# A two-dimensional Fourier step folded by the symmetries of cosine and sine

## The reference, cut to what matters

```python
f_in, f_gate, q_a, kv_a, k_pe, m_gate = split_cols(h_lat @ w_in, EVEN_SPLITS)
...
def fourier_mix(u):
    b, n, _ = u.shape
    f = jnp.fft.fft2(u.reshape(b, n, F_GROUPS, F_GROUP_DIM).astype(jnp.float32), axes=(1, 3), norm='ortho')
    return f.real.reshape(b, n, F_WIDTH).astype(u.dtype)
...
y_l = jnp.concatenate([fourier_mix(f_in) * jax.nn.silu(f_gate),
                       a_l.reshape(b, n, MLA_WIDTH) * jax.nn.silu(m_gate)], axis=-1) @ w_out
```

## Time and profile before

| | us |
|---|---|
| median of 3 runs | 1409.98 |
| lowest, highest | 1406.64, 1414.62 |
| span of the profiled execution (first to last instruction) | 1407.9 |
| PE busy | 1332.3 (95%) |
| DVE busy | 952.2 (68%) |
| ACT busy | 498.6 (35%) |

### The profile page before, as it was taken

One profiled execution on the slowest core, in us unless ns is written; L12 is line 12 of the kernel. 1 busy time (PEld: TensorE's weight loads), 2 busy tenths in 40 slices (PEclk: granted clock), 3 DMA queues, 4 the chain that ended last, 5 costly groups with the idle time before them and its releaser, 6 DMA issues.

```text
span 1407.9 us, 19069 instructions
## 1 busy us (share of the span) xinstructions
PE 1332.3 (95%) x7945; PEld 1087.6 (77%) x7945; DVE 952.2 (68%) x1229; ACT 498.6 (35%) x752; POOL 149.9 (11%) x167
## 2 busy tenths in 40 slices
PE   6999999999999899999998999998999999899997
PEld 2589756546885549889887989886989988789895
DVE  3667857656558576597689666657657778755546
ACT  0422125403246223533232443433354333343432
POOL 2010110000000010012322000002001232100000
PEclk9999999999999999999999999999999999999998
DMA  9453562024331356676774676654557776355551
GB/s 358 150 183 114 176 209 90 19 102 158 126 107 44 121 180 231 195 268 222 278 263 153 236 259 220 202 179 152 188 200 254 269 273 221 122 185 197 184 180 60
DMA packets 104910, 257.95 MB, mean 183 GB/s; under 512 B 8213, under 2 KB 11766, under 8 KB 104570
## 3 DMA queue, kind: packets, MB, share of 16 engines
q1 hardware_dynamic: 80554, 171.78, 36.1%
q0 software_dynamic: 20192, 75.58, 14.8%
q10 hardware_dynamic: 4080, 9.39, 2.0%
HBM read 255.68 MB, written 1.05 MB: 182 GB/s over the span
## 4 chain that ended last, share of the span: by engine, by line
PE 70%; DVE 16%; DMA 4%; ACT 4%; issue 3%; POOL 1%; ACTq 1%; SPq 0%; POOLq 0%; DVEq 0%
PE bank L758 68%; DMA weight_ring<-in_w_in_dram 3%; DVE weights_low L2110 2%; PE bank L918 2%; DMA x<-in_ctx_dram 1%; ACT odd_prob L1694 1%; DVE negated_maxima L2321 1%; POOL inverse_roots L661 1%; ACT weights_high L1521 1%; DVE statistics L2064 1%; ACT even_A L1639 1%; DVE x L2063 1%; DVE xn L2057 1%; DVE x L2552 1%; DVE modulation_sums L1922 1%
## 5 line engine op out<-in xcount | busy, mean ns | idle before, releaser
L2110 DVE TENSOR_TENSOR weights_low<-weight_ring,weights_high 128x2048 fp32r<-128x2048 f32 (+1 forms) x124 | 272.5, 2200 | 227.2 <-ACT weights_high L1521 227.1
L1521 ACT ACTIVATE weights_high<-weight_ring 128x2048 fp32r<-128x2048 f32 (+1 forms) x124 | 227.5, 1836 | 391.2 <-PE bank L758 302.4
L758 PE MATMUL bank<-uT_high,weights_high 128*128 128x256 f32 (+1 forms) x1200 | 341.2, 284 | 8.6 <-DVE weights_low L2110 3.1
L758 PE MATMUL bank<-uT_low,weights_high 128*128 128x256 f32 (+1 forms) x1200 | 339.5, 283 | 0.0
L758 PE MATMUL bank<-uT_high,weights_low 128*128 128x256 f32 (+1 forms) x1200 | 339.4, 283 | 0.0
L758 PEld LDWEIGHTS bank<-uT_high,weights_high 128*128 128x128 f32 (+1 forms) x1200 | 228.3, 190 | 14.1 <-ACT gate_tanh L1835 7.2
L758 PEld LDWEIGHTS bank<-uT_low,weights_high 128*128 128x128 f32 (+1 forms) x1200 | 228.5, 190 | 1.0
L758 PEld LDWEIGHTS bank<-uT_high,weights_low 128*128 128x128 f32 (+1 forms) x1200 | 228.4, 190 | 0.5
L1922 DVE SCALAR_TENSOR_TENSOR modulation_sums<-modulation_ring,silu_c_columns,modulation_sums 128x1024 f32<-128x1024 f32 x112 | 148.7, 1327 | 20.5 <-DMA modulation_ring<-in_w_ada_dram 11.1
L758 PE MATMUL bank<-weights_high,hidden_high 128*128 128x512 f32 x256 | 102.4, 400 | 1.9 <-DVE weights_low L2110 1.9
L758 PE MATMUL bank<-weights_low,hidden_high 128*128 128x512 f32 x256 | 101.8, 398 | 0.0
(11 more groups left out here) (303 smaller groups left out, 2202.5 us busy)
## 6 DMA issues: line engine op xcount, KB each, us to landing
weight_ring<-in_w_in_dram SPq DMA_DIRECT2D x52, 1024.0 KB, 6.7
modulation_ring<-in_w_ada_dram POOLq DMA_DIRECT2D x48, 1024.0 KB, 7.3
weight_ring<-in_w_up_dram SPq DMA_DIRECT2D x32, 1024.0 KB, 5.4
weight_ring<-in_w_down_dram SPq DMA_DIRECT2D x32, 1024.0 KB, 5.0
modulation_ring<-in_w_mod_dram POOLq DMA_DIRECT2D x16, 1024.0 KB, 5.9
weight_ring<-in_o_w_in_dram SPq DMA_DIRECT2D x10, 1024.0 KB, 5.2
weight_ring<-in_w_branch_dram SPq DMA_DIRECT2D x16, 512.0 KB, 3.8
weight_ring<-in_w_o_dram SPq DMA_DIRECT2D x8, 1024.0 KB, 7.0
```

The lines of the kernel that those rows point to most:

```text
L758: return track(pe.matmul(*args, **kw))
L1521: act.activation(ring[:, s, c0:kn * cols], wring[:, slot, c0:kn * cols], ACT.Copy).then_inc(S["high_ready"], 1)
L2110: dve.tensor_tensor(lo[:, s, c0:kn * cols], wring[:, slot, c0:kn * cols], hi[:, s, c0:kn * cols].bitcast(F32), ALU.subtract).then_inc(w_fr ...
```

## The change

Cosine is even and sine is odd in both indices. So (1) f1 computes only 65 cosine columns (0 to 64) and 63 sine columns (1 to 63), 128 together, and ACT writes the others as mirror images, with the sign turned for sine. (2) Tokens t and 256 - t have the same cosine and opposite sine: fin's copy writes tokens 1 to 128 as they are and then 255 down to 128 in reversed order, f1 adds or subtracts the two halves in the accumulator (two products, the second with the sine columns negated), and f2 sums over 128 tokens instead of 256. (3) Token 0 is apart: one product f0 with 8 columns (4 groups times 2 streams), in bank 7; DVE copies it to `dft0` and adds it per partition when it reads f2, one instruction for each stream, since the scalar differs. (4) DVE's `gemv` calls are placed anew: gemv(3, 0) ahead of f2(0), gemv(3, 1) ahead of f2(2), gemv(3, 2), gemv(3, 3) and gemv(4, 0) behind f2(3), and gemv(4, 1..3) behind `mod_columns(3)`. f2 stays in bank 6 alone.

```diff
@@ first_jobs
+        if g == 0:
+            jobs += [(("f0",), last)]
         if g < 4:
-            jobs += [(("f1", g, h), (4, 5)) for h in range(2)]
+            jobs += [(("f1", g), (4, 5))]
...
@@ PE
+            for m in range(4):
+                copied(("fin", m))
+            o = start(("f0",))
+            first_tokens = fT.rearrange("p g s n -> p (g s) n")[:, :, 0]
+            done(product(o[:, 0:8], kE[:, KE_ALL:KE_ALL + P], first_tokens, start=True, stop=True), ("f0",))
             for g in range(5):
                 if g < 4:
-                    copied(("fin", g))
...
+                    o = start(("f1", g))
+                    for s in range(2):
+                        for part in range(2):
+                            ins = product(o[:, P * s:P * s + P], fT[:, g, s, P * part + 1:P * part + P + 1], kE[:, KE_CH + P * part:KE_CH + P * part + P],
+                                          start=(part == 0), stop=(part == 1), skip_group_check=True)
+                    done(ins, ("f1", g))
...
                     for s in range(2):
-                        for i in range(TC):
-                            for part in range(2):
...
+                        for part in range(2):
+                            seq = KE_SEQ + N * part
+                            ins = product(o[:, N * s:N * s + N], dft1[:, (g - 1) % 2, s, P * part:P * part + P],
+                                          kE[:, seq:seq + N], start=(part == 0), stop=(part == 1),
+                                          skip_group_check=True)
@@ ACT
-                copy_out(("fin", m), fT[:, m, :], o[:, :])
+                act.activation(fT[:, m, :, 0:P + 1], o[:, :, 0:P + 1], ACT.Copy)
+                copy_out(("fin", m), fT[:, m, :, P + 1:N + 1], o[:, :, N - 1:P - 1:-1])
...
+                act.activation(dst[:, :, 0:EVENS], o[:, :, 0:EVENS], ACT.Copy)
+                act.activation(dst[:, :, EVENS:P], o[:, :, EVENS - 2:0:-1], ACT.Copy)
+                act.activation(dst[:, :, P + 1:P + EVENS - 1], o[:, :, EVENS:P], ACT.Copy)
+                copy_out(("f1", g), dst[:, :, P + EVENS:2 * P], o[:, :, P - 1:EVENS - 1:-1], scale=-1.0)
@@ DVE
+            link(dve.memset(dft1[:, :, :, P], 0.0))
+            link(dve.memset(dft1[:, :, :, P + EVENS - 1], 0.0))
             low_e("fgate", 0)
...
+            o = ready(("f0",))
+            ins = dve.tensor_copy(dft0, o[:, 0:8])
+            release(ins, ("f0",))
+            copied(("f0",))
             for g in range(4):
-                gemv(3, g)
+                if g % 2 == 0:
+                    gemv(3, g // 2)
...
-                if g == 1:
-                    mod_columns(2, mcol, 0)
-            for q in range(3):
-                gemv(4, q)
+            mod_columns(2, mcol, 0)
+            for q in range(2, 4):
+                gemv(3, q)
+            gemv(4, 0)
             for m in range(4):
                 gated_tile(("mgate", m), 4 + m, eyT[:, 4 + m, :], tanh_e[:, m % 2, :])
             mod_columns(3, mcol, 1, vcol[:, V_NG + KD:V_NG + 2 * KD])
-            gemv(4, 3)
+            for q in range(1, 4):
+                gemv(4, q)
```

54 lines of the change are left out of this document (24 added, 30 removed).

## The result

The changed kernel takes 1422.2 us (median of 4 runs, 1417.9 to 1422.6), the kernel before beside it 1412.1 (4 runs, 1406.6 to 1414.6): a ratio of 1.0076, 95% interval 1.0058 to 1.0095. It is slower by 0.8%. The profiled execution spans 1420.2 us, against 1407.9.

What follows compares the result with a forecast made beforehand. It took DVE, not PE, to pace the stage: 3.8 us gained up to mgate, 6.0 lost behind it and 3.9 lost to PE's lower clock made +6.1 on the median 1409.98, so 1416, range 1405 to 1422.

Steps and rivals of the forecast that it cites:

- f0's copy: On DVE after the low part of mgate: copying f0 was put at 0.2 us, within 0.1 to 0.3.
- The wait of about 5 us: Sign that the forecast is right: PE waits about 5 us in the stage for DVE's reading of f2(0).
- mgate at 148.3: End of the stage: DVE's terms sum to 16.8 us, so mgate starts at 148.3 instead of 152.10, 3.8 us gained.
- half the clock in f2(1): After PE's 6.8 us wait for bank 6, f2(1) probably runs at half the clock: +1.5 us (0 to 1.7).
- Behind mgate: +6.0: From mgate to qb's second half: three late quarters make it 46.3 us against 40.3, 6.0 us lost.
- the ring: Behind mgate: DVE waits for the third late quarter's data, whose slot the first of them frees, 0.7 us (0 to 3).
- the three waits for which the prediction had a term: PE's waits ahead of f2(1), f2(3) and qb's second half lower the clock: +1.5, +0.8 and +1.6, together +3.9 us.
- The 5.0: Clock cost by the Trainium skill's rule, under which all three PE waits cost: 5.0 us instead of 3.9.
- PE's gain arrives: Rival for the stage: PE is at 95%, and 13.6 us come off, giving 1396; chance 0.06.
- The late quarters are hidden: Rival behind mgate: the late quarters do not reach qb and the 3.8 us gain stays, 1406; chance 0.08.
- DVE's pace without falls of the clock: Rival: no wait lowers PE's clock, leaving +2.2 us, 1412; chance 0.12.
- Slower by the ring: Rival behind mgate: last quarter's transfer lands late, clock stays low into kvb, +2 each: +10, 1420; chance 0.14.

Runs made afterwards that it cites:

- e1: The changed kernel with f0 copied out of bank 7 by ACT, ahead of its f1 loop, instead of by DVE; 1415.6 us, ratio 1.0041.
- e12: The changed kernel with f0 written to bank 6 instead of bank 7, still copied by DVE; 1417.7 us, ratio 1.0041.
- e4: The kernel before, without the fold, with only the changed kernel's new places of DVE's gemv quarters; 1417.2 us, ratio 1.0056.
- e6: Against e3: one bank for f1, two for f2, f0 in bank 6, DVE's quarters put off behind the readings of f2; 1401.2 us, ratio 0.9918.
- e10: Folded kernel with e6's quarter places and ACT's copy of f0, but the kernel before's banks, two for f1 and one for f2; 1402.0 us, ratio 0.9933.
- e11: e6 with gemv(4, 2) moved from ahead of the keys' rotation to behind it; 1398.3 us, ratio 0.9899.
- e9: The kernel before, without the fold and with its own banks, but with e6's places of DVE's quarters; 1408.7 us, ratio 0.9973.
- e3: The changed kernel with f0 copied by ACT and DVE's quarters back in the order of the kernel before; 1407.6 us, ratio 0.9988.
- e5: e3 with the banks dealt out the other way, one for f1 and two for f2; 1401.7 us, ratio 0.9939.

## Why the prediction was wrong

It said 1416 (1405 to 1422) and no measurable difference as the likeliest; measured were 1422.2 and slower by 0.76%, with an interval that excludes 0.5%. By its own steps:

**f0's copy: the step that failed.** It was put at 0.2 us, as work of DVE. Its length is right: 0.19 from its start, 132.45, to the first row of the quarter behind it. But f0 lies in bank 7, and so do the sums over the modulation columns: PE could not start these 16 one-column rows until DVE had copied f0, and DVE came to it only behind the low part of mgate, at 132.53. PE had computed f0 at 125.6. The diff names the bank and the code's `start` waits for it, and the prediction even counted bank 6 with this care; of bank 7 it asked only how long the reader takes, not who is queued for it. e1 and e12 give its price, 0.35% each, 4.9 us. The wait of about 5 us that PE was to have for the reading of f2(0) did not come either: PE got to f2(1) late by itself, and it was DVE that waited, 3.82, for f2(0).

**mgate at 148.3.** It came at 155.82, or 154.9 with the start's offset taken off: 6.6 us later. In the working's own terms, from the end of mgate's low part:

| term | predicted | after | e1, f0 copied by ACT |
|---|---|---|---|
| f0's copy, gemv(3, 0), until f2(0) is read | 5.2 | 9.0 (132.45 to 141.46), 3.82 of it idle | 5.0 (132.61 to 137.63) |
| f2(0) read, f2(1) | 3.0 | 4.3 (to 145.79) | 3.3 (to 140.97) |
| f2(1) read, gemv(3, 1) | 5.8 | 5.8 (to 151.61) | 5.8 (to 146.79) |
| f2(2) read | 1.0 | 1.0 (to 152.63) | 1.0 (to 147.81) |
| f2(3) | 1.7 | 3.2 (to 155.82) | 3.2 (to 151.00) |

The first two rows are the missed wait, 3.8 and 1.3. f2(0) was to be ready by 136.8, and the late one-column products and half the clock behind the wait made it 141.4. f2(1) then had to wait until 143.78 for the second stream's one-column products, which the prediction had done at 131; it ran at full clock itself (the row from 142 to 146). Together 5.1, and e1, which takes the wait away, has mgate 5.0 earlier. Beside the wait only the last row is the clock, 1.5 for a predicted 0.8; the 1.5 that the prediction set down for half the clock in f2(1) did not come, neither here nor in e1 or e12. With f0 out of the way the working up to mgate nearly holds: 148.3 and its 2.3 for the clock are 26.0 from the stage's first product, and e1 has 25.2, e12 25.5. That it comes so near is partly luck, since the 1.5 too much for f2(1) stands against 0.7 and 0.3 too little in the last and the second row.

**Behind mgate: +6.0.** 155.82 to 203.60 is 47.8 against 46.3. The mechanism is the one predicted, with its three late quarters in a row, a wait of 0.81 for the ring (0.7 predicted) and two tiles that lay ready. 1.0 of the 1.5 is mgate's first products at half the clock (155.82 to 179.22 where it was 152.10 to 174.47). Then the second half of qb and kvb: +2.8 where +1.6 stood. e4 measured the new places alone: 7.9 us, where the terms (6.0 + 1.6) said 7.6. The start of the second half of qb, 203.60, lies beyond the 196 to 200 that were foretold, mainly because mgate was late.

**The clock.** Of the three waits for which the prediction had a term, it was below full speed behind two, those ahead of f2(3) and of the second half of qb. They cost 1.5 + 1.0 + 2.8 = 5.3, where 0.8 + 1.6 stood. For the third, f2(1), 1.5 stood and nothing was measured; the clock was at 0.50 from 130.7 to 140.9 instead, ahead of it and behind f0's wait (in e1, behind 1.54 of idle and the one-column products, from 129.3 to 136.1). The Trainium skill ("TensorE: Matmul & The Clock Gate", HAM oscillation) says that bursts with waits between them run at half the clock again and again. The rows agree for the long waits of this stage (5.88, 3.85 and 7.26 us of idle). The 5.0 that the prediction worked out by this rule lies near 5.3 partly by luck, since it counts f2(1).

**The sum.** 6.1 was predicted and 13.1 was lost at the attention in the traces. Of the 7.0 between them 5.1 are f0's wait and 1.4 the size of the clock's terms (5.3 for 3.9); the rest is small. The medians lie 10.1 apart, 4.0 more than the forecast's 6.1 and less than f0's wait alone (4.9 by e1). The time itself, 1422.2 for 1416, was missed by 2.1 more: the median before was 1409.98 of three runs when the forecast was made, and is 1412.1 with the fourth.

**The rivals.** *PE's gain arrives* asked for readings that wait for no quarter. That is what e6, e10 and e11 made, and there a part of it arrived: 5.6 us from e9 to e10, and with the new places and banks 1402 to 1398 in all. In the kernel as it was, it did not: its condition, and not only its chance, was read rightly. *The late quarters are hidden* is what e4 excludes. *DVE's pace without falls of the clock* is excluded by the rows at 0.50. *Slower by the ring* had about the right time, 1420, by luck: the transfer landed in 5.45, and the ring took 0.81 where the rival needed 2 more. Its other 2, for the clock from the wait ahead of qb into kvb, it had partly right (2.8 where the sum had 1.6). That a bank is shared was no rival at all, and the range ended, by 0.2 us, too low.

## What to carry to other kernels

A product that is put into a shared bank costs not its reader's length but its reader's place in the queue: look up who uses the bank next and at which time the reader gets to it. When one engine's work is cut in a stage that another paces, ask through which bank the pace is passed on; here the fold was worth 0 to 3.5 us behind one bank with quarters ahead of each reading (e3), and some 6 us once readings came first (e9 to e10). And work that is moved out of a tight stage must be given to a place where its engine waits: the same quarters cost 8 us in one row behind mgate (e4). Spread around the columns of modulation 3 and between the halves of qb they cost little: from mgate to the attention it is 63.6 us in e9, 64.2 in e10 and 66.1 in e6, beside 63.0 in the kernel before and 73.4 in the changed one.

## What the runs showed of the hardware

- Waits among f2's products were followed by half the clock in some places (3.85 in the kernel after, 3.99 in e3, 2.55 in e5) and not in others (2.43 in e3, 2.08 before), and executions of programs that are alike up to there differ (e6 and e11 at 130). One such stretch cost 1 to 3 us here (1.5 in f2(3), 2.8 in the second half of qb and kvb, both in the kernel after), and a difference of that size between two traces is not yet one of the kernels.
- Reading a bank in reversed order cost ACT nothing that shows: 126 columns with a negative step take 0.27, beside 0.28 for 130 forwards.
- A product of 128 columns of plain floats takes little more than half of one with 256 (0.43), namely 0.23 us: in e10 eight of them and four of 256 columns went from 128.97 to 132.56, at a granted clock of 1.00, 3.59 less the 1.72 of the four.
